# A three-block transformer kernel: the modulation's partition sums by transposes and row sums, the linear attention's gate expansion as stacked single-pass products

## What is computed

```
gl = proj[..., 2 * B_KW + 2 * B_VW:].reshape(bn, s, 2, B_RANK)
gate_logit = jnp.einsum('bsnr,nrk->nbsk', gl, gate_w2) + gate_b[:, None, None, :]
log_a = jax.nn.log_sigmoid(gate_logit) / B_TAU
```

## Time and profile before

| | |
|---|---|
| median of three runs | 1845.64 us (1840.9 to 1847.97) |
| the profiled execution | 1845.38 us, of which the span of its engines is 1843.6 us |
| PE busy | 1812.0 us, 98% of the span |
| DVE, ACT, POOL busy | 988.2 us (54%), 735.1 us (40%), 237.1 us (13%) |
| mean granted clock of PE | 0.997 of full speed |

### The profile page before, as it was taken

One profiled execution on the slowest core, in us unless ns is written; L12 is line 12 of the kernel. 1 busy time (PEld: TensorE's weight loads), 2 busy tenths in 40 slices (PEclk: granted clock), 3 DMA queues, 4 the chain that ended last, 5 costly groups with the idle time before them and its releaser, 6 DMA issues.

```text
span 1843.6 us, 24193 instructions
## 1 busy us (share of the span) xinstructions
PE 1812.0 (98%) x9152; PEld 1467.9 (80%) x9152; DVE 988.2 (54%) x1393; ACT 735.1 (40%) x1209; POOL 237.1 (13%) x230
## 2 busy tenths in 40 slices
PE   8999999999999999999999999999999999999999
PEld 6887788888888888887777788788888887876777
DVE  5775466666564444455522468654453466523763
ACT  4434455555232223333542454232232353534541
POOL 2001244332000001000000243000001000101510
PEclk9999999999999999999999999999999999999999
DMA  5333000000343334233222200353226223240001
GB/s 159 92 91 106 32 13 13 1 1 1 103 149 92 98 98 137 92 102 104 59 79 92 69 1 1 124 173 91 91 91 205 92 76 102 88 143 33 23 1 69
DMA packets 102374, 146.77 MB, mean 80 GB/s; under 512 B 4977, under 2 KB 70721, under 8 KB 102032
## 3 DMA queue, kind: packets, MB, share of 16 engines
q1 hardware_dynamic: 95472, 121.45, 21.0%
q0 software_dynamic: 6816, 24.13, 4.0%
HBM read 143.47 MB, written 2.10 MB: 79 GB/s over the span
## 4 chain that ended last, share of the span: by engine, by line
PE 93%; DVE 2%; issue 2%; ACT 1%; POOL 1%; DMA 1%; SPq 0%; ACTq 0%; DVEq 0%; POOLq 0%
PE bk L280 23%; PE bk L282 23%; PE bk L281 23%; PE bk L1099 2%; PE bk L1117 2%; PE bk L1108 1%; PE bk L2857 1%; PE bk L2858 1%; PE bk L2879 1%; PE bk L1015 1%; PE bk L997 1%; POOL work L1523 1%; PE bk L1985 1%; PE bk L1128 1%; PE bk L1159 1%
## 5 line engine op out<-in xcount | busy, mean ns | idle before, releaser
L259 DVE TENSOR_TENSOR wlo<-raw,whi 128x1024 fp32r<-128x1024 f32 x214 | 255.7, 1233 | 360.6 <-ACT whi L253 357.1
L280 PE MATMUL bk<-act_hi,whi 128*128 128x512 f32 x960 | 383.7, 400 | 0.3 <-DVE wlo L728 0.3
L282 PE MATMUL bk<-act_hi,wlo 128*128 128x512 f32 x960 | 380.6, 396 | 0.0
L281 PE MATMUL bk<-act_lo,whi 128*128 128x512 f32 x960 | 380.5, 396 | 0.0
L253 ACT ACTIVATE whi<-raw 128x1024 fp32r<-128x1024 f32 x214 | 216.8, 1054 | 270.5 <-PE bk L282 243.9
L280 PE MATMUL bk<-whi,act_hi 128*128 128x512 f32 x768 | 308.8, 402 | 3.0 <-DVE act_lo L475 1.8
L282 PE MATMUL bk<-whi,act_lo 128*128 128x512 f32 x768 | 304.7, 397 | 0.0
L281 PE MATMUL bk<-wlo,act_hi 128*128 128x512 f32 x768 | 303.4, 395 | 0.0
L280 PEld LDWEIGHTS bk<-act_hi,whi 128*128 128x128 f32 x960 | 180.8, 188 | 48.6 <-issue 4.1
L281 PEld LDWEIGHTS bk<-act_lo,whi 128*128 128x128 f32 x960 | 180.8, 188 | 44.1 <-issue 1.0
L282 PEld LDWEIGHTS bk<-act_hi,wlo 128*128 128x128 f32 x960 | 180.8, 188 | 44.0
(11 more groups left out here) (392 smaller groups left out, 2478.9 us busy)
## 6 DMA issues: line engine op xcount, KB each, us to landing
raw<-in_mlp_w SPq DMA_DIRECT2D x128, 512.0 KB, 4.3
raw<-in_a_w_in SPq DMA_DIRECT2D x32, 512.0 KB, 4.2
work<-in_w_mod POOLq DMA_DIRECT2D x24, 512.0 KB, 4.0
raw<-in_b_w_in SPq DMA_DIRECT2D x24, 512.0 KB, 3.8
raw<-in_w_in SPq DMA_DIRECT2D x14, 512.0 KB, 4.3
raw<-in_a_w_out SPq DMA_DIRECT2D x8, 512.0 KB, 3.9
raw<-in_b_w_out SPq DMA_DIRECT2D x8, 512.0 KB, 4.2
raw<-in_w_out SPq DMA_DIRECT2D x8, 512.0 KB, 3.6
```

What stands on the lines that cost most here:

```text
L259: nc.vector.tensor_tensor(wlo[b][:, hs], raw[hf][:, :], whi[b][:, hs], ALU.subtract).then_inc(w_ready, 1)
L280: nc.tensor.matmul(acc, lhs_hi, rhs_hi, start=first, stop=False, skip_group_check=True)
L281: nc.tensor.matmul(acc, lhs_hi, rhs_lo, start=False, stop=False, skip_group_check=True)
L282: return nc.tensor.matmul(acc, lhs_lo, rhs_hi, start=False, stop=last, skip_group_check=True)
```

## The change

Four things are edited.

1. `pe_mod` transposes the 16 column blocks of `mod_acc` (128 x 128, with `eye`) into the four banks `bk[4]` to `bk[7]`, and `dve_mod` sums over the free axis with four `reduce_sum` of 4 x 128 columns each, before it adds `b_mod`.
2. `pe_b_low` uses gate weights that are repeated three times side by side (96 columns in place of 32), so `gl` appears on partitions 0 to 31, 32 to 63 and 64 to 95. ACT copies the 96 rows, rounded to fp32r, to `gl_rows`, and DVE (in `dve_b_in`) turns the third copy into the rest (true value less rounded). The weights `gate2` hold hi, lo and hi on the same partitions, so one product over 98 partitions sums hi·hi, hi·lo and lo·hi; partitions 96 and 97 hold ones against the bias as hi and lo. `pe_b_la` is now one fp32r product for each tile.
3. To prepare that, POOL loads the small matrices three times and the bias twice, ACT does five copies in `act_b_gate_weights` where it did one, and DVE four operations in `dve_b_gate_weights` where it did one. The buffers lie in `b_cum` and `b_las`, so the copy of the constants `cum` moves behind the eight gate tiles.
4. Several semaphores are merged into counters (`Steps`, `softplus`); the operations around them are the same. These hunks are left out below.

```diff
@@ -1686,16 +1706,19 @@
             pe.wait_ge(mod_sum, 18 * (third + 1))
             for n in range(8):
                 for w in range(2):
-                    mm = nc.tensor.matmul(bk[4][:, 4 * n + 2 * w:4 * n + 2 * w + 2], mod_acc[:, w, n * P:n * P + P], ones[:, 0:2],
-                                          start=True, stop=True, skip_group_check=True)
+                    c = (n % 2 * 2 + w) * P
+                    mm = nc.tensor.transpose(bk[4 + n // 2][:, c:c + P], mod_acc[:, w, n * P:n * P + P], eye[:, :])
             mm.then_inc(mod_mm, 1)
             pe.wait_ge(acc_free, 2 * FS[name] + 32)
 
         def dve_mod(dve, third):
             dve.wait_ge(mod_mm, third + 1)
             r = VEC["b_mod"][0] + 8 * third
-            nc.vector.tensor_tensor(modc[:, 8 * third:8 * third + 8, :], bk[4][:, 0:32].rearrange("p (n w) -> p n w", w=4)[:, :, 0::2],
-                                    cols[:, r:r + 8].unsqueeze(2).broadcast_to([P, 8, 2]), ALU.add).then_inc(mod_read, 1)
+            m = modc[:, 8 * third:8 * third + 8, :]
+            for i in range(4):
+                nc.vector.reduce_sum(m[:, 2 * i:2 * i + 2, :].rearrange("p n w -> p (n w)"), chunks(bk[4 + i]), AX_X).then_inc(mod_col, 1)
+            dve.wait_ge(mod_col, 4 * (third + 1))
+            nc.vector.tensor_tensor(m, m, cols[:, r:r + 8].unsqueeze(2).broadcast_to([P, 8, 2]), ALU.add).then_inc(mod_read, 1)
 
 
         b_qT = arena[:, 0:2048].rearrange("p (n s) -> p n s", n=BH)
@@ -1709,9 +1732,19 @@
                           ("S0", BDV), ("S1", BDV), ("rs", S), ("gl", 8)], start=4096)
         b_masks = BB["masks"][:, 0:LEVELS * P // 4].bitcast(U8).rearrange("p (l s) -> p l s", l=LEVELS)
         b_masks_f = work[:, 2048:2048 + LEVELS * P]
-        BG = carve(work, [("glT", S), ("w2", 2, S), ("t", 2, S), ("cum", 2048)], start=4352)
+        BG = carve(work, [("w2", 2, S), ("t", 2, S), ("cum", 2048)], start=4864)
+        cum_row, las_row = b_cum[:, :, :, :].rearrange("p d l s -> p (d l s)"), b_las[:, :, :, :].rearrange("p i c s -> p (i c s)")
+        gw3 = cum_row[:, 0:2 * KT * 96].rearrange("p (i k n) -> p i k n", i=2, k=KT)
+        gl_rows = cum_row[:, 2 * KT * 96:2 * KT * 96 + S]
+        gate2 = las_row[:, 896:896 + 2 * S].rearrange("p (n k) -> p n k", n=2)
+        bias_rows = BG["t"][96:98, :, :]
+        gw3_in = gw_raw.unsqueeze(2).broadcast_to([P, KT, 3, 32])
+
+        def gw3_part(i):
+            return gw3[:, i, :, :].rearrange("p k (q n) -> p k q n", q=3)
+
         B = {n: sem("b_" + n) for n in (
-            "w_loaded gate_loaded cum_loaded cum_ready masks_loaded masks_ready gate_set w_hi w_ready gl_mm gl la_mm absd expd ln la "
+            "w2_hi w2_lo gl_lo w_loaded gate_loaded cum_loaded cum_ready masks_loaded masks_ready gate_set w_hi w_ready gl_mm gl la_mm softplus la "
             "las_hi las_lo e_mm exp gl_col zk zq qd kd sc st k_turned k_tok u s o_done o_sq o_sum o_ln o_rs of1 o_out").split()}
 
         def b_e(d, slot):
@@ -1732,30 +1765,31 @@
 
         def pool_b_load(pool):
             pool.wait_ge(mod_mm, 1)
-            nc.gpsimd.memset(BG["glT"][0:33, :], 1.0).then_inc(B["gate_set"], 1)
-            nc.gpsimd.memset(BG["w2"][0:33, :, :], 0.0).then_inc(B["gate_set"], 1)
-            pool.wait_ge(B["gate_set"], 2)
+            nc.gpsimd.memset(BG["w2"][0:96, :, :], 0.0).then_inc(B["gate_set"], 1)
+            pool.wait_ge(B["gate_set"], 1)
             pool.dma_start(gw_raw, a["b_w_in"][0, :, 3072:3104].rearrange("(k p) n -> p k n", p=P)).then_inc(B["w_loaded"], 16)
-            for n in range(2):
-                pool.dma_start(BG["w2"][RANK * n:RANK * n + RANK, n, :], a["b_gate_w2"][0, n]).then_inc(B["gate_loaded"], 16)
-            pool.dma_start(BG["w2"][32:33, :, :], a["b_gate_b"]).then_inc(B["gate_loaded"], 16)
+            for q in (0, 32, 64):
+                for n in range(2):
+                    pool.dma_start(BG["w2"][q + RANK * n:q + RANK * n + RANK, n, :], a["b_gate_w2"][0, n]).then_inc(B["gate_loaded"], 16)
+            for q in (96, 97):
+                pool.dma_start(BG["w2"][q:q + 1, :, :], a["b_gate_b"]).then_inc(B["gate_loaded"], 16)
             pool.dma_start(BG["cum"], a["k_cum"]).then_inc(B["cum_loaded"], 16)
             pool.dma_start(b_masks_f, a["k_masks"]).then_inc(B["masks_loaded"], 16)
 
         def pe_b_la(pe, t):
             n, st = t // ST, t % ST
             if t == 0:
-                pe.wait_ge(B["gl"], 1)
-                pe.wait_ge(B["gate_loaded"], 16 * 3)
+                pe.wait_ge(B["gl_lo"], 1)
+                pe.wait_ge(B["w2_lo"], 3)
             if t >= 2:
                 pe.wait_ge(B["la"], t - 1)
-            nc.tensor.matmul(bk[6 + t % 2][:, :], BG["glT"][0:33, st * P:st * P + P], BG["w2"][0:33, n, :],
+            nc.tensor.matmul(bk[6 + t % 2][:, :], gl_rows[0:98, st * P:st * P + P], gate2[0:98, n, :],
                              start=True, stop=True).then_inc(B["la_mm"], 1)
 
         def pe_b_low(pe):
             pe.wait_ge(B["w_ready"], 1)
             for kt in range(KT):
-                mm = mm3(bk[4][0:32, :], gw_hi[:, kt, :], gw_lo[:, kt, :], act_hi[:, kt, :], act_lo[:, kt, :],
+                mm = mm3(bk[4][0:96, :], gw3[:, 0, kt, :], gw3[:, 1, kt, :], act_hi[:, kt, :], act_lo[:, kt, :],
                          kt == 0, kt == KT - 1)
             mm.then_inc(B["gl_mm"], 1)
 
@@ -1793,19 +1827,16 @@
             act.wait_ge(B["la_mm"], t + 1)
             if t >= 2:
                 act.wait_ge(B["la"], t - 1)
-            nc.scalar.activation(tb, bk[6 + t % 2][:, :], ACT.Abs).then_inc(B["absd"], 1)
-            act.wait_ge(B["absd"], t + 1)
-            nc.scalar.activation(tb, tb, ACT.Exp, scale=-1.0).then_inc(B["expd"], 1)
-            act.wait_ge(B["expd"], t + 1)
-            nc.scalar.activation(tb, tb, ACT.Ln, bias=1.0).then_inc(B["ln"], 1)
+            nc.scalar.activation(tb, bk[6 + t % 2][:, :], ACT.Abs).then_inc(B["softplus"], 1)
+            act.wait_ge(B["softplus"], 3 * t + 1)
+            nc.scalar.activation(tb, tb, ACT.Exp, scale=-1.0).then_inc(B["softplus"], 1)
+            act.wait_ge(B["softplus"], 3 * t + 2)
+            nc.scalar.activation(tb, tb, ACT.Ln, bias=1.0).then_inc(B["softplus"], 1)
 
         def act_b_in(act):
             log_exp_table()
             act.wait_ge(B["gl_mm"], 1)
-            act.wait_ge(B["gate_set"], 2)
-            nc.scalar.activation(BG["glT"][0:32, :], bk[4][0:32, :], ACT.Copy).then_inc(B["gl"], 1)
-            act.wait_ge(B["cum_loaded"], 16)
-            nc.scalar.activation(b_cum[:, :, :, :].rearrange("p d l s -> p (d l s)"), BG["cum"], ACT.Copy).then_inc(B["cum_ready"], 1)
+            nc.scalar.activation(gl_rows[0:96, :], bk[4][0:96, :], ACT.Copy).then_inc(B["gl"], 1)
             for k2 in range(2):
                 for b in range(2):
                     for j in range(2):
@@ -1816,6 +1847,8 @@
                     split_hi(act, next_pair("b_qk", k2), b)
                     act_b_la(act, 4 * k2 + 2 * b)
                     act_b_la(act, 4 * k2 + 2 * b + 1)
+            act.wait_ge(B["cum_loaded"], 16)
+            nc.scalar.activation(cum_row, BG["cum"], ACT.Copy).then_inc(B["cum_ready"], 1)
             for k2 in range(2):
                 for b in range(2):
                     for j in range(2):
@@ -1841,15 +1874,29 @@
 
         def act_b_gate_weights(act):
             act.wait_ge(B["w_loaded"], 16)
-            nc.scalar.activation(gw_hi, gw_raw, ACT.Copy).then_inc(B["w_hi"], 1)
+            nc.scalar.activation(gw3_part(0), gw3_in, ACT.Copy).then_inc(B["w_hi"], 1)
+            nc.scalar.activation(gl_rows[96:98, :].rearrange("p (c s) -> p c s", c=ST), ones[96:98, :].unsqueeze(1).broadcast_to([2, ST, P]),
+                                 ACT.Copy).then_inc(B["w2_hi"], 1)
+            act.wait_ge(B["gate_loaded"], 16 * 8)
+            nc.scalar.activation(gate2[0:96, :, :], BG["w2"][0:96, :, :], ACT.Copy).then_inc(B["w2_hi"], 1)
+            nc.scalar.activation(gate2[96:98, :, :], BG["w2"][96:98, :, :], ACT.Copy, scale=eye[96:98, 96:97]).then_inc(B["w2_hi"], 1)
+            nc.scalar.activation(bias_rows.bitcast(F32R), BG["w2"][96:98, :, :], ACT.Copy).then_inc(B["w2_hi"], 1)
 
         def dve_b_gate_weights(dve):
             dve.wait_ge(B["w_hi"], 1)
-            nc.vector.tensor_tensor(gw_lo, gw_raw, gw_hi, ALU.subtract).then_inc(B["w_ready"], 1)
+            nc.vector.tensor_tensor(gw3_part(1), gw3_in, gw3_part(0), ALU.subtract).then_inc(B["w_ready"], 1)
+            dve.wait_ge(B["w2_hi"], 4)
+            nc.vector.tensor_tensor(gate2[32:64, :, :], BG["w2"][32:64, :, :], gate2[32:64, :, :], ALU.subtract).then_inc(B["w2_lo"], 1)
+            nc.vector.tensor_tensor(bias_rows, BG["w2"][96:98, :, :], bias_rows, ALU.subtract).then_inc(B["w2_lo"], 1)
+            dve.wait_ge(B["w2_lo"], 2)
+            nc.vector.scalar_tensor_tensor(out=gate2[96:98, :, :], in0=bias_rows, scalar=eye[96:98, 97:98], in1=gate2[96:98, :, :],
```

(58 more changed lines are left out.)

7 lines of the change are left out of this document (4 added, 3 removed).

## The result

The changed kernel takes 1831.66 us in the median of five runs (1831.31 to 1831.81), against 1845.36 before (five runs, 1840.9 to 1847.97). The ratio is 0.9928, with a 95% interval from 0.9916 to 0.9939: 13.7 us, or 0.7%. The profiled execution has a span of 1829.3 us (1843.6 before) and a mean clock of 0.999 (0.997).

A forecast was written before the change was run, and what follows sets the result against it. PE bounds the kernel, with 93% of the chain. Gains of 8.36 (modulation) and 6.4 (gate tiles) less 0.15 (wait) make 14.6 us: 1845.38 becomes 1830.8, plus 0.3 to the median gives 1831.0 us; range 1826.5 to 1836.

The forecast's parts named there:

- The modulation blocks: PE's two modulation blocks: 11.86 us with their slow tails becomes 3.5 us as transposes at full clock, a gain of 8.36 us.
- The gate tiles: Four pairs of gate tiles on PE: each 2.12 us becomes 0.5 us, a gain of 6.4 us in all.
- The wait ahead of the first: PE's first gate tile also waits for DVE's subtraction: 0.15 us added, 0.7 us were there no cover.
- The preparation in "down0": DVE's four operations in place of one stay hidden, with 1.1 us to spare; ACT's five copies count nothing.
- The cover of the bank's eviction: Behind "up0", ACT frees the last banks by 696.5, transposes end near 697.6; the shorter block still covers it.
- The moved copy and POOL's loads: ACT's 1.89 us copy moves behind the last gate tile; POOL's loads become eleven from six: no cost from either.
- (b): Rival: the clock falls behind the transposes too, leaving 3.8 us of tails: 1834.8 us, chance 0.10.
- (c): Rival: longer waits in "down0" or before the first gate tile, tiles nearer 0.43 us: 1832.5 to 1835.5 us, chance 0.09.
- (d): Rival: a 98-partition gate product takes as long as the two instructions before, 6.4 us not gained: 1837.4 us, chance 0.06.
- (e): Rival: slower, as DVE's two-partition operations in "down0" take far longer and hold PE: 1857 us at 9 us each, chance 0.03.
- The lower end of the range: 1826.5 us: the sum less a run scatter of 3.5 us and a further microsecond for the clock's tails.

The follow-up runs named there:

- the three executions: Three more profiled executions of the kernel before, unchanged: 1848.4, 1840.78 and 1844.35 us.
- e7_spread: Kernel before, each modulation block's 32 thin instructions spread, eight behind each token tile of the next layer's first slab: 1843.69 us, ratio 0.9992.
- e9_spread_cover: Kernel before with thin products spread, but each block's first eight put ahead of PE's wait for the last freed bank: 1841.46 us, ratio 0.9984.
- e1_mod_only: Kernel before with the modulation edit alone (transposes and row sums), gate tiles as they were: 1836.99 us, ratio 0.9957.
- the second execution: Second of three more profiled executions of the unchanged kernel before: 1840.78 us.
- e4_transposes_x3: Changed kernel with each block's sixteen transposes done three times over, 48 in a row: 1839.03 us.
- the two added loads: Changed kernel with two or six extra unused row sums on DVE in "down0": 1832.13 us with two, 1834.92 us with six.
- e6_dve_plus6: Changed kernel with six extra unused row sums in DVE's preparation in "down0": 1834.92 us.

## Why the prediction was right

The forecast was 1831.0 us, and 1831.66 was measured.

- *The modulation blocks*: 1.75 us each, clock at 1.00, as in its rows of sixteen transposes; 8.36 us in the profiled pair. The mechanism, that the tail and the second block's slowness are a fallen clock caused by the thin run, is shown by the three executions and by `e7_spread` and `e9_spread_cover`. But the term was taken from one execution, in which 4.7 of its 8.36 us were falls that vary from 0 to 6.3 us. Against an execution without falls the edit gives 3.66 us by this sum, against one with both 9.96. Two profiles without a fall, of the kernel before (1840.78) and of `e1_mod_only` (1836.52), bear the lower figure out: they differ by 4.3 us, 0.35 of it ahead of the first block (695.78 against 695.43), which leaves 3.9. The forecast time hangs less on this than the term does, since the falls are in the execution that the sum starts from as well. From the second execution the same working gives 1840.78 - 3.66 - 6.4 + 0.15 = 1830.9. But the prediction then adds the distance from its execution to the median, and a median that contains falls has nothing to say of a kernel without them: here that step was 0.3 us, because the profiled execution happened to sit near the median (1845.38 against 1845.64 of the three runs then known). From the second execution it would have been 4.9, and the forecast 1835.7. That it came out at 1831.0 is luck in this step.
- *The gate tiles*: 1.64 us a pair for a forecast 1.6, so 0.24 us for a product; the row of four fp32r products was the right neighbour, the lone one at 0.43 was not.
- *The wait ahead of the first*: 0.25 us for 0.15.
- *The preparation in "down0"*: hidden, with 1.5 us to spare for a forecast 1.1; the two added loads show that both the margin and what lies behind it are real.
- *The cover of the bank's eviction*, named as holding by a microsecond, is shown from the other side: without it `e7_spread` loses 1.9 us in its chain.
- *The moved copy and POOL's loads*: nothing, as forecast. ACT's idle time ahead of the second eviction of "b_r" goes from 5.02 to 1.88 us, and PE's one wait for these evictions is 0.7 us before and after.
- Of the rivals, (b) is refuted by `e4_transposes_x3`, at three times the length; (c) and (d) by the profile, (e) by the operations on two partitions, 1.2 to 1.3 us each. Its price was also reckoned too high: three operations of 9 us would come to some 1853 us, not 1857, since their 1.2 us each are in the sum already, and only two of them are on two partitions. The stretch behind the transposes in the earlier trace rows is 3.3 us, not 3.5. Neither touches the sum.
- *The lower end of the range* was argued from a spread of 3.5 us around the sum. The spread did not carry over: it belonged to the code that was removed.

What stays open: what in the gate edit makes the wait for POOL in block B 0.3 us longer, what makes the clock fall in one execution and not in another, and in how many runs a wait such as that of `e6_dve_plus6` brings a fall.

## What to carry to other kernels

When the runs of a kernel on one core lie several microseconds apart, read several profiles before one is used to price a term: the same instructions cost 3.6 us in one execution and 6.7 in another, by the clock alone. A run of products with two moving columns between dense stretches is a place where that happens; make it shorter, break it up with dense products, or turn it into transposes and row sums on an idle engine. In these runs the transposes gained by being half as many instructions and by keeping the clock up. And before such a block is moved, see what it covers: here it hid a bank's eviction, worth about a microsecond each time.

## What the runs showed that was not expected

A fall of the clock is not tied to the code alone: of the four profiles of the kernel before, one has no fall at the blocks, one has one and two have two. It cost 3.15 us at four of their eight blocks, 1.5 at one and nothing at three. A wait of 2.1 us within dense work was followed by one in the profile of `e6_dve_plus6`. Forty-eight transposes in a row, 5.24 us, brought none in the profile, and none of ten runs has the time of a full one. And a plain float32 product of 512 columns takes 0.95 us on PE (1.91 for two), four times the 0.24 us of one in fp32r from these buffers.
